# The cache's compression moves into the gathers of tile 0, and two thirds of w_ada into the input projection

## What is computed

```
sh1, sc1, g1, sh2, sc2, g2 = split(silu(c) @ w_ada + b_ada, 6)      # c: 9 condition rows; w_ada 2048 x 12288
h  = rmsnorm(x, norm_mix) * (1 + sc1) + sh1
p  = h @ w_in                             # q, kv of three branches, gates, qkv and z of the delta rule
# samples, compressed branch: 8 x 16 pages of 128 past tokens, found by page_table
rows = cache_cmp_kv[page_table]
hid  = gelu(einsum('bnlshd,slde->bnshe', blocks(rows, 32) + cmp_pe, cmp_w1) + cmp_b1)
ckv  = einsum('bnshe,sed->bnshd', hid, cmp_w2)       # one compressed k and v per 32 tokens
o  = [sparse attention (compressed, selected, window) | gated delta rule]
x  = x + g1 * (o @ w_out)
h  = rmsnorm(x, norm_ffn) * (1 + sc2) + sh2
# expert retrieval: each token picks 8 x 16 of 16384 experts, in blocks of 128 tokens
act = gelu(h . u_tab[eid]);   x = x + g2 * sum(gate * act * v_tab[eid])
```

## Time and profile before

| | us |
|---|---|
| median of 3 runs | 2960.16 (2957.48 to 2960.38) |
| the profiled execution | 2967.48 |
| its span | 2965.9 |
| busy TensorE / VectorE / ScalarE / GpSimd | 1929.3 / 1183.7 / 388.2 / 883.0 |
| moved by DMA | 919.76 MB, 310 GB/s on the mean |

### The profile page before, as it was taken

The page is one execution under the profiler, slowest core; times in us unless marked ns, Lnnn a source line. Parts: engine busy times, 40 slices in busy tenths (PEclk is TensorE's granted clock), DMA queues, the critical chain, the costliest instruction groups (busy, mean ns, idle before and its releaser), DMA issues.

```text
span 2965.9 us, 31791 instructions
## 1 busy us (share of the span) xinstructions
PE 1929.3 (65%) x11949; PEld 1237.4 (42%) x11949; DVE 1183.7 (40%) x2088; ACT 388.2 (13%) x815; POOL 883.0 (30%) x726
## 2 busy tenths in 40 slices
PE   6898989999988779840000888767265316545673
PEld 4666657888868458840000556312021101111020
DVE  3222221003336543489999012604867770000014
ACT  1222220000132232200000010211021100000011
POOL 2212100000000110028888322335764363221233
PEclk8988989999989668975555899977587757666775
DMA  8999976444240074669999999999999989999997
GB/s 295 342 359 339 350 247 193 153 141 147 85 114 1 27 247 145 214 227 418 418 422 422 418 419 416 416 417 386 400 404 384 410 342 413 402 345 377 421 404 324
DMA packets 296110, 919.76 MB, mean 310 GB/s; under 512 B 22318, under 2 KB 152418, under 8 KB 221818
## 3 DMA queue, kind: packets, MB, share of 16 engines
q0 software_dynamic: 88624, 603.34, 50.4%
q1 hardware_dynamic: 187346, 295.19, 28.5%
q10 hardware_dynamic: 20028, 19.75, 2.0%
HBM read 909.57 MB, written 17.21 MB: 312 GB/s over the span
## 4 chain that ended last, share of the span: by engine, by line
PE 37%; DMA 32%; POOL 14%; DVE 7%; issue 7%; POOLq 1%; ACT 1%; ACTq 1%; SPq 0%; DVEq 0%; PEldq 0%
DMA sb_ring<-in_peer_v_dram,sb_modT 16%; PE ps L545 12%; POOL sb_ring L2539 12%; DMA sb_ring<-in_peer_u_dram,sb_dist 7%; PE ps L2466 3%; PE ps L373 2%; DMA sb_ring<-in_cache_sel_kv_dram 2%; DMA sb_ring<-in_w_out_dram 2%; DVE sb_ring L2153 2%; PE ps L1906 2%; PE ps L356 2%; DMA sb_ring<-in_cache_cmp_kv_dram 2%; PE ps L341 1%; DMA sb_pT<-in_cmp_w_dram 1%; PE ps L2050 1%
## 5 line engine op out<-in xcount | busy, mean ns | idle before, releaser
L2153 DVE SCALAR_TENSOR_TENSOR sb_ring<-sb_ring,sb_pT 128x2048 f32<-128x2048 f32 x264 | 602.7, 2295 | 144.4 <-DMA sb_ring<-in_peer_u_dram,sb_dist 99.0
L2539 POOL DMA_INDIRECT sb_ring<-in_peer_u_dram,sb_dist x256 | 497.9, 1945 | 377.2 <-DVE sb_ring L2153 161.9
L2466 PE MATMUL ps<-sb_ring,sb_xT 128*32 128x512 f32 x2048 | 340.1, 761 | 156.9 <-DMA sb_ring<-in_peer_v_dram,sb_modT 154.1
L2539 POOL DMA_INDIRECT sb_ring<-in_peer_v_dram,sb_modT x256 | 248.2, 970 | 612.7 <-PE ps L2466 587.4
L545 PE MATMUL ps<-sb_hT,sb_ring 128*128 128x264 f32 x1664 | 370.8, 386 | 0.0
L545 PEld LDWEIGHTS ps<-sb_hT,sb_ring 128*128 128x128 f32 x1664 | 316.0, 190 | 54.4 <-issue 0.4
L2450 PE MATMUL ps<-sb_ident,sb_levels 128*128 128x128 f32 x2 | 0.9, 462 | 334.0 <-DVE sb_levels L2162 334.0
L2466 PEld LDWEIGHTS ps<-sb_ring,sb_xT 128*32 128x32 f32 x2048 | 52.5, 123 | 381.2 <-DMA sb_ring<-in_peer_v_dram,sb_modT 313.6
L1714 PE MATMUL ps<-sb_work,sb_pT 128*64 128x512 f32 x160 | 98.9, 705 | 97.2 <-ACT sb_work L1605 66.6
L217 POOL DMA_DIRECT2D sb_ring<-in_cache_cmp_kv_dram x128 | 69.1, 540 | 304.0 <-issue 304.0
L2450 PEld LDWEIGHTS ps<-sb_ident,sb_levels 128*128 128x128 f32 x2 | 0.4, 182 | 334.7 <-DVE sb_levels L2162 316.9
(11 more groups left out here) (582 smaller groups left out, 2721.7 us busy)
## 6 DMA issues: line engine op xcount, KB each, us to landing
sb_ring<-in_w_ada_dram SPq DMA_DIRECT2D x48, 2048.0 KB, 12.0
sb_ring<-in_w_in_dram SPq DMA_DIRECT2D x26, 2048.0 KB, 8.4
sb_ring<-in_cache_cmp_kv_dram POOLq DMA_DIRECT2D x128, 256.0 KB, 6.0
sb_ring<-in_w_out_dram SPq DMA_DIRECT2D x19, 1024.0 KB
sb_ring<-in_peer_wq_dram SPq DMA_DIRECT2D x18, 1024.0 KB
sb_ring<-in_w_out_dram SPq DMA_DIRECT2D x8, 2048.0 KB, 23.2
sb_ring<-in_peer_wq_dram SPq DMA_DIRECT2D x8, 2048.0 KB, 9.0
sb_pT<-in_peer_wq_dram SPq DMA_DIRECT2D x14, 1024.0 KB
```

The costliest lines, as they stand in the source:

```text
L2153: dve.scalar_tensor_tensor(R3(rows), R3(rows), 1.0, h2r[t] if t < NT else R3(h2w), ALU.mult, ALU.mult, accum_out=(dots if t < NT else dots ...
L2466: mm = pe.matmul(bank(G % 2)[32 * q:32 * q + 32, :], w, rows[:, 512 * q:512 * q + 512], start=j == 0, stop=j == last)
L2539: pool.indirect_dma_start(rbuf[e % NBUF], None, io["peer_u" if kind == "u" else "peer_v"][0], bass.IndirectOffsetOnAxis(index, 0)).then_in ...
```

## The change

**Start.** The loop is gone. SP (`sp_mods`) loads the first 16 of 48 w_ada items, which are cut in another way: 4 blocks of rows by 1024 columns, so runs of 4 KB. TensorE (`pe_mods`) does their 8 matmuls each (L213), the transposes of each finished group of four (L223), and between the groups the transposes of x; then the norm's sums and the hidden layer's bias. ScalarE's queue loads w1. Only the modulations that the first norm needs get their bias here, the others after the projection.

**Input projection.** After each of the 16 w_in items TensorE does two further w_ada items, and after every second one the transposes of the last finished group; one sequence of ring slots serves both (`in_seq`, `ada_seq`). The first convolution transposes wait for the last modulation.

**Tile 0's dots.** Transposes, moves, hidden layer, gelu and second layer of the compression now stand here: `pe_cmp` between the transposes of tile 0's expert numbers and those of its weights, `act_cmp` before the dots' gelu. ScalarE does all moves (L2382). Pages pass in pairs through the four quarters of ring slot 3; SP loads the first eight and then the even pages, ScalarE the odd ones in line after a move (L2296, L2297). w1 is loaded again in six parts into whatever is free (L2311), the last part after the gates of tile 0; w2 too. The hidden layer of a sample comes after the second page of the next, its second layer after the sixth. The first two w_out blocks of `sp_rest` wait for the last page transpose, the next two for the last hidden layer.

```diff
+        ADA_FIRST, ADA_ALL, IN_ITEMS, QKV_ITEMS = 16, 48, 16, 10
+        ada_seq = lambda n: n if n < ADA_FIRST else ADA_FIRST + 3 * ((n - ADA_FIRST) // 2) + 1 + n % 2
+        in_seq = lambda m: ADA_FIRST + 3 * m if m < IN_ITEMS else ADA_FIRST + 3 * IN_ITEMS + m - IN_ITEMS
...
+        def slot_free(sp, i):
+            if i >= RING:
+                used, count = USERS[i - RING]
+                sp.wait_ge(sem(used), count)
+
+        def load_ada(sp, n):
+            g, kq = divmod(n, 4)
+            i = ada_seq(n)
+            slot_free(sp, i)
+            sp.dma_start(ring[:, i % RING, :].rearrange("p (k n) -> p k n", k=4),
+                         io["w_ada"][0].rearrange("(k p) n -> p k n", p=P)[:, 4 * kq:4 * kq + 4, 1024 * g:1024 * g + 1024]).then_inc(full[i % RING], 16)
...
-            pe_project(pe, G_IN, 0, 16, hT3)
+            for m in range(IN_ITEMS):
+                i = in_seq(m)
+                pe_item(pe, i % RING, seq_full(i), 2 * m, hT3)
+                if m % 2 == 0 and m:
+                    pe_ada_T(pe, 3 + m // 2)
+                for n in range(2):
+                    pe_ada(pe, ADA_FIRST + 2 * m + n)
+            pe_ada_T(pe, 11)
...
                 elif m < 2:
-                    sp.wait_ge(sem("proj_sum"), 8 + 84)
+                    sp.wait_ge(sem("page_T"), CMP_PAGES)
                 else:
-                    sp.wait_ge(sem("samp_ready"), 1)
+                    sp.wait_ge(sem("hid_sum"), 2 * NB)
...
+        def sp_cmp(sp):
...
+            for n in range(4):
+                load_cmp(sp, n)
+            for n_, (to, s, l0, l1) in enumerate(w1_parts):
+                if n_ == len(w1_parts) - 1:
+                    sp.wait_ge(sem("work_clear"), 1)
+                sp.dma_start(to, io["cmp_w1"][0, s, l0:l1].rearrange("l d e -> d l e")).then_inc(sem("w1_back"), 16)
...
+            for i in range(4, CMP_PAGES // 2):
+                sp.wait_ge(sem("page_T"), 2 * i - 6)
+                load_cmp(sp, 2 * i)
+
+        def pe_cmp(pe):
+            def page_turn(n):
+                i, pp = divmod(n, 2)
+                if pp == 0:
+                    pe.wait_ge(full[i % RING], cmp_base[i % RING] + 32 * (i // RING + 1))
+                if n >= 2:
+                    pe.wait_ge(sem("page_moved"), n - 1)
+                for c in range(4):
+                    mm = pe.transpose(bank(n % 2)[:, c * P:(c + 1) * P], cmp_slot[i % RING][:, pp * 512 + c * P:pp * 512 + (c + 1) * P], ident[:])
+                mm.then_inc(sem("page_T"), 1)
...
+            for n in range(CMP_PAGES):
+                b, pp = divmod(n, PAGES)
+                page_turn(n)
+                if b and pp == 1:
+                    hidden(b - 1)
+                if b and pp == 5:
+                    compressed(b - 1)
...
+            for n in range(CMP_PAGES):
+                b, pp = divmod(n, PAGES)
+                act.wait_ge(sem("page_T"), n + 1)
+                if b and pp == 0:
+                    gelus(b - 1)
+                for s in range(2):
+                    mv = act.activation(XTw[s][:, :, 4 * pp:4 * pp + 4, :], bank(n % 2)[:, 256 * s:256 * s + 256].rearrange("p (h n l) -> p h n l", h=KVH, n=4), ACT.Copy)
+                mv.then_inc(sem("page_moved"), 1)
+                if n % 2 == 1 and n + 8 < CMP_PAGES:
+                    load_cmp(act, n + 8)
+                if b and pp == 6:
+                    kept(b - 1)
```

More of the change, by code:

```diff
@@ L186, in bank @@
+        seq_full = lambda i: 16 * (i // RING + 1)
+        ada_banks = lambda g: (2, 3) if g in (0, 2) else (4, 5)
         def bank(i):
             return ps[:, i, :]
-        def sp_compress(sp):
-            sp.dma_start(pagesb[:], io["page_table"].rearrange("(a b) c -> a (b c)", a=1)).then_inc(sem("pages_in"), 16)
[L193 to L206, removed]
@@ new lines, in load_ada, with pe_ada @@
+        def load_ada(sp, n):
[4 more added lines that the diff above has]
+                         io["w_ada"][0].rearrange("(k p) n -> p k n", p=P)[:, 4 * kq:4 * kq + 4, 1024 * g:1024 * g + 1024]).then_inc(full[i % RING], 16)
+        def pe_ada(pe, n):
+            g, kq = divmod(n, 4)
+            i = ada_seq(n)
+            pe.wait_ge(full[i % RING], seq_full(i))
+            if kq == 0 and g >= 2:
+                pe.wait_ge(sem("modrow_moved"), 2 * (g - 1) if g < 4 else 2 * g)
+            w = ring[:, i % RING, :].rearrange("p (k n) -> p k n", k=4)
+            for cb in range(2):
+                for k in range(4):
+                    mm = pe.matmul(bank(ada_banks(g)[cb])[32 * k:32 * k + 32, :], cT[:, (4 * kq + k) * 32:(4 * kq + k) * 32 + 32],
+                                   w[:, k, 512 * cb:512 * cb + 512], start=kq == 0, stop=kq == 3)
+            mm.then_inc(sem("mod_part"), 1)
@@ L398, in dve_setup @@
+            for g in range(4):
+                for kq in range(4):
+                    pe_ada(pe, 4 * g + kq)
+                if g:
+                    pe_ada_T(pe, g - 1)
+                if g < 3:
+                    pe_x(pe, g)
+            for q in range(4):
+                pe_norm(pe, 1, q, hT3)
+            pe_hid_bias(pe)
+            pe_ada_T(pe, 3)
         def dve_setup(dve):
@@ L2407, in act_window @@
             act_exp(act, 0)
+            act_cmp(act)
             gelu(0)
@@ L2581, in _ @@
         def _(pe):
-            for stage in (pe_setup, pe_compress, pe_in, pe_delta_norm, pe_delta_gates):
+            for stage in (pe_setup, pe_mods, pe_in, pe_delta_norm, pe_delta_gates):
                 stage(pe)
@@ L2592, in _ @@
         def _(dve):
-            for stage in (dve_setup, dve_compress, dve_in, dve_conv, dve_delta_gates):
+            for stage in (dve_setup, dve_mods, dve_in, dve_conv, dve_delta_gates):
                 stage(dve)
```

415 lines of the change are left out of this document (187 added, 228 removed).

## The result

The changed kernel takes 2823.7 us as the median of four runs (2815.55 to 2829.07), the kernel before 2960.1 in the same comparison: a ratio of 0.9539, 95% interval 0.9511 to 0.9567. The forecast was 2835, with 2815 to 2865 as its own range. The profiled execution took 2819.42 us, its span is 2817.6.

What follows compares the result with a forecast made beforehand. Transfers bound the opening loop and tile 0's dots, TensorE the projection. An earlier convolution (−226 us) and longer dots (+100) give −126: 2841.5 from the profiled 2967.5, 2835 us as a median, own range 2815 to 2865 (8 in 10: 2805 to 2900).

Steps and rivals of the forecast that it cites:

- Both halves of the mechanism: Whole kernel: the convolution starts 226 us earlier; tile 0's dots grow by 100 us; together −126 us.
- What bounds each stage: Old loop: transfers, TensorE close behind; input projection: TensorE alone, DMA at 0.48; tile 0's dots: transfers, DMA at 0.99.
- The start: Before the projection: 16 w_ada items land near 110 us; projection starts at about 150 us (143 to 165), was 457.
- The projection: Input projection: 228.0 us plus 57.1 for w_ada items, 16.8 for transposes, 7 for waits: 309 us, TensorE still the bound.
- The margin of 8%: Projection: per w_in item and two w_ada items TensorE needs 18.9 us, the transfers 17.4 us.
- The dots: Tile 0's dots: pages 86 us, last part of w1 3.6, w_out rows 10; sum +100 us (88 to 112).
- The pages: Tile 0's dots: 120 pages, 31.5 MB, take 86 us at 366 GB/s (77 to 94).
- The chain beneath: Compression under tile 0's dots: 44.5 us per sample, 360 us in all, ending 56 us before the dots; hidden if under 52.
- Projection bound by transfers: Rival, input projection: mixed transfers cost 3 us more per triple, 16 triples lose 48 us: 2883; chance 10%.
- Stalled issues on ScalarE: Rival, tile 0's dots: ScalarE's page issues stall; gain gone from 3.9 us per issue, 3421 at 11.6 us; chance 4%.
- The chain as the bound: Rival, tile 0's dots: compression outlasts them, hidden layer at 1.2 GHz, perhaps late pages: 2870 to 2918; chance 21%.
- Better than forecast: Rival, whole kernel: pages at 409 GB/s, start at 143 and a projection without waits: 2808; chance 8%.

## Why the prediction was right

Both halves of the mechanism held, and the sum was 11 us too high as a median. Some of its parts were further off than the sum. Step by step:

*What bounds each stage* held: all three stages have the bound that it named, and the two that got work without becoming longer (TensorE and ScalarE in the dots, transfers in the projection) are those it named too.

*The start (150 forecast, 146.4).* The last item came at 111 us as counted (110). The 164 ns estimated for 4 KB measured 169. The step behind it was a little shorter: the norm's sums took 7.2 us and not 10.2, the hidden layer's bias with its copies 6.0 and not 8.6. The sums are a matter of luck: two of the seven runs whose start is that of the changed kernel, or differs from it in the run length alone, have them at 9.9 us, with the projection at 152 to 153.

*The projection (309 forecast, 305.2).* The rates held nearly: an item of w_in took 14.44 us among the others (14.25 before), most groups of transposes 1.70 us and not 2.1, and waits and small steps came to some 2 us and not 7. The margin of 8% sufficed for runs of 2 KB as well.

*The dots (+100 forecast, +92.9).* The run without page loads splits it. The pages were the term that was mis-sized: 79 us, near the lower of its bounds (77), where I had taken 86 from the loop's w_ada. The rest, w1 and w_out, cost 14 us (330.4 − 316.3), and I had 13.6. That this term fits is in part luck: of w1 not only the last part fell into the dots but four of six, 2.6 MB and not 1, yet leaving them out shortened the dots by only 3 us.

*The chain beneath (360 forecast, 378).* The total was near and its parts were not. ScalarE was quicker: without page loads a sample took 31.9 us (hidden layers from 1128.6 to 1352.1, seven samples apart), so about 1 us per page where I had counted 1.47 with the loads; a load costs ScalarE 0.37 us at its issue and not 0.89. The hidden layer took 15.0 to 16.5 us (18 taken). In their place stood what I had not counted: 45.7 us behind w1, and some 8 us of waits for pages in each sample (110.5 − 45.7 over eight). That the total came near is luck: what was too dear and what was left out mostly cancelled. The forecast of 56 us to spare was 31 us, and either of two small disturbances (8 x 7.3 us of TensorE, or one queue for the pages) used it up.

The Trainium skill's "TensorE: Matmul & The Clock Gate", "HAM oscillation — how this bites in real kernels", says that a burst of matmuls behind a wait for transfers starts cold. The rows agree: behind the waits for pages the first hidden layer starts with 18 records in 3.58 us, 199 ns each, and ends with 78 in 8.87 us, 114 ns; the granted clock is 0.50 (1.2 GHz) from 1148.9 to 1151.9 us and 1.00 (2.4 GHz) from 1152 on. The other seven start slow as well. That a layer of this length would then stay cold to its end, 29.4 us, was my reading and does not stand in the section; the rows refute it. The slow start costs about 1.5 us of this layer, not 14.7. In the run without page loads, where no layer but the first comes behind such a wait, six of the eight take 14.46 us.

*The rivals.* Projection bound by transfers: refuted at both run lengths. Stalled issues on ScalarE: no issue of a page there was longer than 0.374 us; SyncE had the stall, 16.2 us at 1090.18. The chain as the bound: true from 31 us on. *Better than forecast* was nearer on the pages' price (77 us against 86, measured 79).

## What to carry to other kernels

Sort the stages by their bound, and pay for bytes in stages that have idle transfers, for matmuls and moves where the transfers are full; 67 MB woven into the projection cost 76 us, nearly all of it their matmuls and transposes, while 39 MB put into a stage with full transfers cost all of their 93 us. In a stage whose transfers are full, price every added byte near the stage's own rate (here 400 GB/s against 421), and count all loads that land there, not only the ones that are issued there. Hidden work has a threshold: look at which queue its loads stand in, and behind what.

## What the hardware showed unexpectedly

A load's time to land beside a full stream depended on its queue, not only on its bytes: a page issued at 1090.18 on the queue that still held short packets of w1 landed 43 us later, while pages on two queues came in pairs every 3.84 us and on one queue every 6.3 us, at the same total rate (413 and 414 GB/s from 1150 to 1450 us). It fits that the queues take turns at the engines, one run of a page (2 KB) against one row of a gather (8 KB): pages on one queue would then get 2 parts of 10, an estimated 83 GB/s of the 414, and on two queues 4 of 12, 138 of the 413. What they got, 512 KB in 6.33 and in 3.84 us, is 83 and 137. That it is turns and not another rule with the same shares no run here shows; one with pages in longer runs would test it.

That page packets of 2 KB would cost so little more per byte than gathers was not to be seen before: the loop's own rate for 2 KB was 366 GB/s, the pages' in the dots 400, and the gathers' alone 421.
